# Expert rows gated on leaving PSUM and scattered with an add onto stored residual rows, in place of two gathered rows a token added at the end

## The reference

```python
x = x + hierarchical_moe(rmsnorm(x, norm2_g), ...)      # x is x1
return rmsnorm(x, final_g)

# inside hierarchical_moe, t = rmsnorm(x1), 32 experts, two of them for each token
combine = sum over the 2 chosen experts of one_hot(expert_id) * gate
for e in range(32):
    y = (silu(t @ e_gate[e]) * (t @ e_up[e])) @ e_down[e]
    out = out + combine[:, e:e + 1] * y
```

## Time and profile before

| | |
|---|---|
| median of 3 runs | 893.04 us |
| the profiled execution, its own time | 892.98 us |
| its span | 891.0 us |
| TensorE busy | 771.9 us, 87% of the span |
| VectorE, ScalarE, GpSimd busy | 42%, 34%, 37% |
| bytes moved by DMA | 160.2 MB, mean 180 GB/s |
| mean granted TensorE clock | 0.941 of full speed |

### The profile page before, as it was taken

One profiled execution on the slowest core, in us unless ns is written; L12 is line 12 of the kernel. 1 busy time (PEld: TensorE's weight loads), 2 busy tenths in 40 slices (PEclk: granted clock), 3 DMA queues, 4 the chain that ended last, 5 costly groups with the idle time before them and its releaser, 6 DMA issues.

```text
span 891.0 us, 13079 instructions
## 1 busy us (share of the span) xinstructions
PE 771.9 (87%) x5022; PEld 641.3 (72%) x5022; DVE 373.1 (42%) x767; ACT 302.0 (34%) x539; POOL 329.7 (37%) x313
## 2 busy tenths in 40 slices
PE   3999999999977888999973599999999999999700
PEld 2788888866654554787873599999998899999600
DVE  5540000046768885412238233343333333333266
ACT  6211112145558887202220233333333333333222
POOL 2432256435556771501110123443433333442134
PEclk9999999979999999999995699999999999999955
DMA  8451112000010002426358189999999999996194
GB/s 273 108 151 48 47 48 71 1 0 1 2 48 0 1 1 76 137 69 219 113 172 300 38 258 335 351 349 351 348 349 350 347 342 347 350 352 231 40 370 195
DMA packets 111238, 160.21 MB, mean 180 GB/s; under 512 B 8304, under 2 KB 88656, under 8 KB 111072
## 3 DMA queue, kind: packets, MB, share of 16 engines
q1 hardware_dynamic: 104800, 142.78, 47.9%
q0 software_dynamic: 6400, 16.92, 5.9%
HBM read 144.99 MB, written 18.87 MB: 184 GB/s over the span
## 4 chain that ended last, share of the span: by engine, by line
PE 75%; DVE 9%; ACT 6%; DMA 4%; issue 3%; POOL 1%; SPq 1%; POOLq 0%; ACTq 0%; DVEq 0%
PE ps L768 26%; PE ps L583 6%; PE ps L585 6%; PE ps L584 6%; PE ps L788 3%; PE ps L787 3%; PE ps L792 3%; PE ps L623 3%; PE ps L759 2%; PE ps L648 2%; PE ps L707 2%; PE ps L709 2%; PE ps L708 2%; PE ps L664 2%; PE ps L670 2%
## 5 line engine op out<-in xcount | busy, mean ns | idle before, releaser
L768 PEld LDWEIGHTS ps<-xT,wg 128*128 128x128 f32 x1024 | 121.6, 195 | 5.9 <-ACT xT L1016 2.3
L768 PE MATMUL ps<-xT,wg 128*128 128x96 f32 x1024 | 121.4, 278 | 1.8 <-ACT xT L1016 1.8
L768 PE MATMUL ps<-xT,wu 128*128 128x96 f32 x1024 | 119.6, 275 | 0.0
L768 PEld LDWEIGHTS ps<-xT,wu 128*128 128x128 f32 x1024 | 116.9, 192 | 0.0
L1388 DVE TENSOR_TENSOR wdlo<-wd,wdhi 128x2048 fp32r<-128x2048 f32 x32 | 73.4, 2292 | 63.0 <-ACT wdhi L1036 63.0
L583 PE MATMUL ps<-hThi,whi 128*128 128x512 f32 x224 | 88.3, 394 | 4.2 <-DVE hTlo L1086 4.2
L585 PE MATMUL ps<-hThi,wlo 128*128 128x512 f32 x224 | 87.7, 392 | 0.0
L584 PE MATMUL ps<-hTlo,whi 128*128 128x512 f32 x224 | 87.7, 391 | 0.0
L1584 POOL COPY tokc<-tok 80x1 int32 (+1 forms) x32 | 54.1, 1689 | 42.7 <-DVE tok L1369 30.7
L1597 POOL COPY destc<-dest 80x1 int32 (+1 forms) x32 | 5.7, 178 | 166.7 <-DVE ysb L1380 166.7
L1536 POOL TENSOR_SCALAR pswa<-pswa,esum 128x384 f32<-128x384 f32 (+1 forms) x48 | 55.5, 1165 | 31.8 <-DVE esum L1173 31.4
(11 more groups left out here) (194 smaller groups left out, 1415.4 us busy)
## 6 DMA issues: line engine op xcount, KB each, us to landing
wg<-in_expert_w_gate SPq DMA_DIRECT2D x32, 1024.0 KB, 8.9
wu<-in_expert_w_up SPq DMA_DIRECT2D x32, 1024.0 KB, 12.7
wd<-in_expert_w_down SPq DMA_DIRECT2D x32, 1024.0 KB, 6.0
y<-expert_rows SPq DMA_DIRECT2D x16, 512.0 KB, 9.5
wraw<-in_w_in SPq DMA_DIRECT2D x14, 512.0 KB, 3.9
xin<-in_x SPq DMA_DIRECT2D x8, 512.0 KB, 5.6
xres<-in_x SPq DMA_DIRECT2D x16, 256.0 KB, 3.0
h_rows<-h SPq DMA_DIRECT2D x8, 512.0 KB, 2.7
```

Source lines behind the costliest of these rows:

```text
L768: mm = nc.tensor.matmul(ps[:, bank, f * COLS:(f + 1) * COLS], w[:, k, c0:c0 + P], xTu[:, k, :], start=(k == 0), stop=(k == KT - 1))
```

## The change

- `expert_rows` (2048 rows) is replaced by `residual_rows` (1024 + 80). SyncE stores each tile of `x1` there (`store_x1`), ahead of the `h2` store.
- The lists of gates, `ggate`, are made as the lists of rows are: VectorE rewrites the 16 `tile_hot` matrices with the gates in them, and TensorE multiplies them by `row_hot` again.
- `dest` now holds the token's row, and for a place not filled a spare row 1024 + place, so that every scatter writes 80 rows.
- POOL copies the expert's column of `ggate` to `gatec` (`gate_of`), once the evacuations of e-2 are done. ScalarE and VectorE multiply by it in their evacuations.
- The scatter's DMA adds (`compute_op=ALU.add`), and waits for the scatter before it to land (`y_put`); the first waits for the stores of `x1`.
- The last stage loads one tile of 128 rows into `xs` (in place of two) and has no `add_rows`.

```diff
+            def store_x1(t):
+                sp.wait_ge(x1_done, TT + t + 1)
+                sp.dma_start(sum_d[t * P:(t + 1) * P, :], x1[:, t, :]).then_inc(x1_put, 16)
+
             def store_h2(t):
+                store_x1(t)
...
-                sp.dma_start(y0[t][:], y_d[t * P:(t + 1) * P, :]).then_inc(yc_in[t], 16)
-                sp.dma_start(y1[t][:], y_d[S + t * P:S + (t + 1) * P, :]).then_inc(yc_in[t], 16)
+                sp.dma_start(xs[t][:], sum_d[t * P:(t + 1) * P, :]).then_inc(yc_in[t], 16)
...
+            for c in range(2 * TT):
+                pe.wait_ge(gate_hots, c + 1)
+                mm = nc.tensor.matmul(ps[0:CAP, 7, 0:LT], row_hot[:, c, :], tile_hot[:, c, :], start=(c == 0), stop=(c == 2 * TT - 1))
+            mm.then_inc(gate_mm, 1)
...
-                nc.scalar.copy(ysb[par][:, 0:512], ps[0:CAP, 4 + 2 * par, :]).then_inc(y_a, 1)
+                act.wait_ge(gate_col, e - 1)
+                nc.scalar.mul(ysb[par][:, 0:512], ps[0:CAP, 4 + 2 * par, :], gatec[par][:, 0:1]).then_inc(y_a, 1)
...
             for t in range(TT):
-                act.wait_ge(c_sum, 2 * (t + 1))
-                nc.scalar.activation(fo[t][:], x1[:, t, :], ACT.Square, ...
+                act.wait_ge(yc_in[t], 16)
+                nc.scalar.activation(fo[t][:], xs[t][:], ACT.Square, ...
...
+            dve.wait_ge(tok_done, 2)
+            nc.vector.tensor_scalar(dest[:], tok[:], dvals[0:CAP, 2 * TT:2 * TT + 1], None, ALU.min).then_inc(tok_done, 1)
+            for c in range(2 * TT):
+                v.tensor_scalar(tile_hot[:, c, :], misc[:, 12:12 + LT], tile[:, c:c + 1], gates[:, c // TT, c % TT:c % TT + 1],
+                                ALU.is_equal, ALU.mult).then_inc(gate_hots, 1)
+            dve.wait_ge(gate_mm, 1)
+            nc.vector.tensor_copy(ggate[:], ps[0:CAP, 7, 0:LT]).then_inc(gate_set, 1)
...
-                nc.vector.tensor_copy(ysb[par][:, 512:1024], ps[0:CAP, 5 + 2 * par, :]).then_inc(y_v, 1)
+                dve.wait_ge(gate_col, e - 1)
+                nc.vector.tensor_scalar(ysb[par][:, 512:1024], ps[0:CAP, 5 + 2 * par, :], gatec[par][:, 0:1], None, ALU.mult).then_inc(y_v, 1)
...
-            def add_rows(t):
-                dve.wait_ge(yc_in[t], 32)
-                for k, y in enumerate((y0[t], y1[t])):
-                    nc.vector.scalar_tensor_tensor(out=x1[:, t, :], in0=y[:], scalar=gates[:, k, t:t + 1], in1=x1[:, t, :],
-                                                   op0=ALU.mult, op1=ALU.add).then_inc(c_sum, 1)
-                    dve.wait_ge(c_sum, 2 * t + k + 1)
...
+            def gate_of(it, u):
+
+                f = it * RING + u
+                first = isinstance(it, int)
+                if not first or u >= 2:
+                    pool.wait_ge(y_a, f - 1)
+                    pool.wait_ge(y_v, f - 1)
+                col = ggate[:, f:f + 1] if first else ggate[:, bass.ds(f, 1)]
+                gp.tensor_copy(gatec[u % 2][:], col).then_inc(gate_col, 1)
...
                 pool.wait_ge(idx_d, f + 1)
-                gp.indirect_dma_start(y_d, bass.IndirectOffsetOnAxis(ap=destc[par][:].bitcast(U32), axis=0), ysb[par][:], None,
-                                      bounds_check=bound(bound_y, 2 * S - 1), oob_is_err=False).then_inc(y_put[par], 16)
+                if isinstance(it, int) and u == 3 and it == 0:
+                    pool.wait_ge(x1_put, 16 * TT)
+                else:
+                    pool.wait_ge(y_put[1 - par], 16 * (it * 2 + (u - 4) // 2 + 1))
+                gp.indirect_dma_start(sum_d, bass.IndirectOffsetOnAxis(ap=destc[par][:].bitcast(U32), axis=0), ysb[par][:], None,
+                                      bounds_check=bound(bound_y, S + CAP - 1), oob_is_err=True, compute_op=ALU.add).then_inc(y_put[par], 16)
...
             with pool.Fori(1, N_EXP // RING) as it:
                 for u in range(RING):
                     gather(it, u)
                     scatter(it, u)
+                    gate_of(it, u)
```

More of the change, by code:

```diff
@@ L117, in encoder @@
     h2_d = nc.dram_tensor("h2_rows", [S, D], F32).ap()
-    y_d = nc.dram_tensor("expert_rows", [2 * S, D], F32).ap()
+    sum_d = nc.dram_tensor("residual_rows", [S + CAP, D], F32).ap()
     with ExitStack() as ctx:
@@ L217, in encoder @@
         dest = at("dest", [CAP, LT], I32, W + 48 * KB)
+        ggate = at("ggate", [CAP, LT], F32, V + 8192 + 3072 + 512)
         tok = at("tok", [CAP, LT], I32, W + 48 * KB + 256)
         tokc = [at(f"tokc{i}", [CAP, 1], I32, W + 48 * KB + 704 + 32 * i) for i in range(2)]
+        gatec = [at(f"gatec{i}", [CAP, 1], F32, W + 48 * KB + 832 + 32 * i) for i in range(2)]
         destc = [at(f"destc{i}", [CAP, 1], I32, W + 48 * KB + 768 + 32 * i) for i in range(2)]
@@ L229, in encoder @@
         xT = [at(f"xT{i}", [P, KT, COLS], F32, TMP + 3072 * i) for i in range(2)]
-        y0 = [at(f"y0{i}", [P, D], F32, H + 8192 * i) for i in range(TT)]
-        y1 = [at(f"y1{i}", [P, D], F32, H + 8192 * i + 4096) for i in range(TT)]
+        xs = [at(f"xs{i}", [P, D], F32, H + 4096 * i) for i in range(TT)]
         fo = [at(f"fo{i}", [P, D], F32, W + 4096 * i) for i in range(TT)]
@@ L332, in encoder @@
         yc_in = [sem(f"yc_in{i}") for i in range(TT)]
-        c_sum = sem("c_sum")
+        x1_put = sem("x1_put")
+        gate_hots = sem("gate_hots")
+        gate_mm = sem("gate_mm")
+        gate_set = sem("gate_set")
+        gate_col = sem("gate_col")
         c_sq_done = sem("c_sq_done")
@@ L811, in down_of @@
             def down_of(e, slot, par, early):
+                if early:
+                    pe.wait_ge(gate_set, 1)
                 if not early:
@@ L1066, in _ @@
                         act.wait_ge(y_put[0], j * 16 + 16 * (N_EXP // 2))
-                        nc.scalar.copy(ysb[0][:, 0:512], ps[0:CAP, 4, :]).then_inc(v_ya, 1)
+                        act.wait_ge(v_idx, 3 * j + 3)
+                        nc.scalar.mul(ysb[0][:, 0:512], ps[0:CAP, 4, :], gatec[0][:, 0:1]).then_inc(v_ya, 1)
             for t in range(TT):
-                act.wait_ge(c_sum, 2 * (t + 1))
-                nc.scalar.activation(fo[t][:], x1[:, t, :], ACT.Square, scale=D ** -0.5, accum_out=stat[:, 0, t:t + 1]).then_inc(c_sq_done, 1)
+                act.wait_ge(yc_in[t], 16)
+                nc.scalar.activation(fo[t][:], xs[t][:], ACT.Square, scale=D ** -0.5, accum_out=stat[:, 0, t:t + 1]).then_inc(c_sq_done, 1)
         @block.vector
@@ L1564, in _ @@
                 gp.memset(xg[i][:], 0.0).then_inc(xg_zero, 1)
-            pool.wait_ge(tok_done, 2)
+            pool.wait_ge(tok_done, 3)
             pool.wait_ge(xg_zero, 2)
@@ L1625, in _ @@
                         pool.wait_ge(v_yv, j + 1)
-                        gp.indirect_dma_start(y_d, bass.IndirectOffsetOnAxis(ap=destc[0][:].bitcast(U32), axis=0), ysb[0][:], None,
-                                              bounds_check=bound(bound_y, 2 * S - 1), oob_is_err=False).then_inc(y_put[0], 16)
+                        gp.indirect_dma_start(sum_d, bass.IndirectOffsetOnAxis(ap=destc[0][:].bitcast(U32), axis=0), ysb[0][:], None,
+                                              bounds_check=bound(bound_y, S + CAP - 1), oob_is_err=True, compute_op=ALU.add).then_inc(y_put[0], 16)
             for t in range(TT):
```

19 lines of the change are left out of this document (12 added, 7 removed).

## The result

| | before | after |
|---|---|---|
| median of 4 runs each, on one chip | 892.82 us (891.31 to 894.35) | 1003.77 us (1002.0 to 1011.95) |
| the profiled execution | 892.98 us | 1003.99 us |
| its span | 891.0 us | 1002.0 us |
| TensorE busy | 771.9 us | 820.6 us |
| mean granted TensorE clock | 0.941 | 0.909 |

The ratio of the means is 1.1261, with a 95% interval of 1.1196 to 1.1325: slower, by 110.9 us between the medians. The direction is right, the size is not: the loss is over twice the 46.5 us that were forecast.

A forecast was written before the change was run, and what follows sets the result against it. TensorE, never waiting from 530 to 836 us, was taken to set the time. 892.98 + 60 (late gathers) + 0.2 (ahead of the loop) - 13.7 (the end) = 939.5 us, range 908 to 984.

The forecast's parts named there:

- The wait moves the gather behind the evacuation: Expert loop: POOL's new wait delays the next gather by one expert; 26 stalls of 2.3 us cost 60 us (42 to 86).
- I take 7.1: Loop: us from the gather's issue to its landing, chosen between 6.9 and 7.4, with ends of 6.4 and 8.1.
- TensorE's clock: Rival, loop: a gap of 2.3 us lowers the clock for part of each period, 2.5 us more an expert; 1005, chance 0.05.
- a clock under 1.00 from 530 us on: Sign that the forecast is wrong: TensorE's granted clock below full speed from 530 us on.
- The adding scatter costs nothing while the gather sets the period: Loop: DMA needs 11.5 to 12.4 us an expert, under the gather's 12.85, so the add costs nothing.
- DMA as the bound, without the gather: Rival, loop: gathers in time, DMA at 11.5 to 12.4 us an expert sets the period; 890 to 915, chance 0.03.
- Ahead of the loop: Before the expert loop: stores of x1 cost nothing, the gate lists' work is mostly hidden; 0.2 us counted.
- The end: After the last experts: chained scatter landings of 4.5 us, then tiles at 2.06 us; saves 13.7 us (7 to 21).
- the blocked one: Last stage: POOL's first operation of the next tile runs beside VectorE's finish (1.28 us) and ends with it.

## Why the prediction was wrong, by its own steps

**The wait moves the gather behind the evacuation: right.** The gather was to be issued 1.4 us after the evacuation and is (1.36). POOL waits for `ysb` ahead of `gatec`, and TensorE's idle time is ended by `xg`. The wait alone, put into the kernel before, costs 125.2 us; taken off the gather in the changed kernel, it gives back 112 to 114. What is left then, some 11 us in the loop, is the load of the add, which does not show while the wait stands.

**"I take 7.1": a mis-sized term.** The landing was 7.7 us as a median, within the ends of 6.4 and 8.1 but above both rows between which 7.1 was taken, about midway between the 7.4 of expert 3's gather and the first scatter's 8.1. The reason given for going below 7.4, that with a longer period less is left of the loads before, has no support: with a DMA share down from 0.97 to 0.82 the gather became slower, and with quarter loads ahead of it it took 5.4. By the filled gap the delay is 3.2 us, where 2.3 were forecast: 26 times 0.9 is 23 us. Of the 0.9 the landing makes 0.6; another 0.2 is a term that the sum did not have, the slower start of the transposes behind a stop (0.88 us in place of 0.66).

**TensorE's clock: the step that failed.** The sum left it at full speed, and the slower clock stood among the rivals with a chance of 0.05 and outside the range. That rival's time, 1005, is what came, 1003.77, but not by its own terms: it had 2.5 us an expert, where 1.4 to 1.5 were measured, and the rest came from the later gather. That the two agree is luck. 26 times 1.4 is 36 us. With the 23 above, 939.5 + 23 + 36 = 998.5; a first gap at expert 4 (3.28, since there are 27 waits, not 26) makes it 1001.8. What misled was the row of 402 to 446 us: its gaps add up to 1.1 us in 44, and it says nothing of a gap of two or three microseconds. The row that does was at hand: 260 to 265 us, with a clock of 0.66, was put down to ten us with much idle time, while the clock was at 1.00 up to 260 and its fall stands right behind one gap of 2.12 us:

```profile
255.22 0.70 PE L629 MATMUL ps<-kb,qb 64*128 64x256 f32 x4
260.17 0.86 PE L664 MATMUL ps<-ptna,vtok 128*64 128x128 f32 x8 [2.12 <-ACT ptna L400]
260.97 1.22 PE L629 MATMUL ps<-kb,qb 64*128 64x256 f32 x4
```

Four products of the same kind took 0.70 us ahead of the gap and 1.22 behind it. (Shorter idle times lie ahead of this gap as well, so these rows do not show that it alone made the fall.) A second gap, of 2.16 us ahead of 272.70, was followed by a fall too; one of 3.08 us ahead of 350.50 was not. The stall that was forecast, 2.3 us, is of that size. So a slow clock behind some of the stalls was no matter of 0.05, and a price for it belonged in the sum or at least in the range. Among the signs of being wrong the prediction did name it: a clock under 1.00 from 530 us on.

**The adding scatter costs nothing while the gather sets the period: right.** With and without the add the changed kernel takes the same time. The size was near too: 11.5 to 12.4 us an expert were forecast for DMA as the bound, and once the wait is gone the transposes follow at 11.5 and 11.9. The rival "DMA as the bound, without the gather" gave 890 to 915; the kernel with four buffers took 890.07. It had a chance of 0.03 because it needs gathers in time, and with the wait in place they were not; it is the reason why taking the wait away gains so little over the kernel before. One figure of that step was off: q0's bytes are 0.52 MB an expert and not 0.59 (13.74 MB in 280 us of 10.55 each), which puts its ends near 11.7 and 12.7 in place of 11.5 and 12.4. That is still under 12.85 and changes nothing in the sum.

On its load, the q0 share of 16.4% without the add and 23.6% with it is measured with gathers in both. If the scatters are 80 of the 144 rows of an expert and the gathers cost the same in both, their part without the add is 9.1 points, and with it 16.3: 1.8 times, an estimate. The Trainium skill (Collectives: The Full Stack, The bandwidth ceiling) has the rate halved by the second source read; these two kernels agree with it nearly.

**Ahead of the loop: right.** The first transposes begin at 498.92, 0.5 us later than in the earlier trace rows; 0.2 was forecast.

**The end: right, 13.1 us for a forecast of 13.7.** The landings were 5.04 and 5.23 where 4.5 was taken, the pitch 2.04 where it was 2.06, and the first operation of POOL beside `finish` takes 1.31 us (0.24 where nothing runs on VectorE, at 980.81), as the blocked one was expected to. The terms' errors (0.5 and 0.7 for the landings, 0.3 for the tile's load) are partly set off by the last store (4.9 for 5.2) and by one tile of shorter pitch (1.76).

## What to carry to other kernels

A copy of one column can cost 12% if its wait stands ahead of something urgent in the queue of an engine: count what is queued behind a new wait, and try its place in the order before adding buffers. When a change opens gaps of a few microseconds on TensorE in a loop, price the clock together with the gap, not as an unlikely extra; here it made some 30% of the loop's loss, and filling the gap with idle products took 34 us back. And when a wait is taken away, look for the limit that it had covered: here the weight loads, which the scatter's add had made late.

## What was not expected of the hardware

**The clock behind a gap.** Stretches of the changed kernel behind a gap of 2.86 us, one of 1.75, and two pieces behind one of 3.33:

```profile
725.00:728.00 3.00, 3.00 (x13) 2.29 (x14) 0.00 (x0) 0.80 (x1) 0.00 (x0) 0.50 1.09 279
711.40:714.00 2.60, 2.60 (x17) 1.95 (x18) 0.00 (x0) 0.80 (x1) 0.00 (x0) 1.00 1.14 334
740.54:742.54 2.00, 2.00 (x13) 1.47 (x14) 0.00 (x0) 0.80 (x1) 0.00 (x0) 0.82 1.11 308
742.54:745.54 3.00, 3.00 (x9) 1.89 (x8) 0.00 (x0) 0.00 (x0) 0.00 (x0) 0.55 0.41 89
```

The lower level is 0.50 of full speed, 1.2 GHz, and the fall comes at the gap's end or some microseconds into the work behind it. Of the 27 transposes that waited, 8 were followed by full speed for the next 5 us, behind gaps of 0.45 to 2.94 us, and behind 19 the clock fell, after gaps of 2.27 to 4.73. So between 2.3 and 2.9 us the gap's length alone did not decide: 2.63 us was followed by the fall at 592.63 and by none at 698.82. In the kernel with the wait alone the shortest gap behind which the clock fell was 2.06 us (684.29). In the two kernels whose gaps stayed at 1.80 us or less (ten filler products, and the quarter loads), the transposes behind all 48 of them took 0.87 or 0.88 us.

**The landing of an indirect gather went more by what was issued just ahead of it than by the mean load.** It took 4.0 us with little left to load, 5.4 with quarter loads at a DMA share of 0.68, 6.9 between loads at 0.97, and 7.7 to 8.0 just behind three fresh loads at 0.75 to 0.82 (the changed kernel, the one with the wait alone, and the one without the add).

**An adding scatter is dearer in three ways.** Its issue holds POOL for 1.43 us and not 0.92, behind the loop, with the weight loads done, it lands in 4.9 to 5.2 us and not 3.3 to 3.9 (the earlier trace rows and the kernel without the add), and by the estimate above its DMA work is about 1.8 times.

**SyncE's issue becomes slow when the loads fall behind.** In the kernel with four buffers, at a DMA share of 1.07, this issue of a load of 1 MB took 6.53 us:

```profile
785.86 6.53 SPq L508 DMA_DIRECT2D wu<-in_expert_w_up  x1
```

In the changed kernel the same issue took 0.53 us at 703.60. The share alone does not tell the cases apart: from 600 to 800 us the longest issue of the kernel before took 1.40 us at shares of 1.03 and 1.04, and that of the kernel with four buffers and no add 3.35 us at 1.05 and 1.06.
